# The keys' products of the mLSTM state placed directly behind the value products, in a two-layer hybrid encoder step

## The reference, cut to what matters

```
S   = einsum(q, k) * exp(D - m_t)
num = w_inter * einsum(C, q) + einsum(S, v)
den = w_inter * einsum(n, q) + sum(S)
h   = num / max(|den|, exp(-m_t))
w_s = exp(b_last - b + logi - m_new)
C_new = decay * C + einsum(w_s, v, k)
n_new = decay * n + einsum(w_s, k)
```

## Time and profile before

| what | value |
|---|---|
| median of 3 runs | 2419.7 us (2417.2 to 2423.41) |
| profiled execution, device time | 2419.36 us |
| its span, first to last instruction | 2417.6 us |
| granted TensorE clock, mean | 0.999 |
| PE busy | 2390.9 us (99%) |
| DVE, ACT, POOL busy | 1542.3 (64%), 1082.9 (45%), 524.5 us (22%) |
| mean DMA traffic | 111 GB/s |

### The profile page before, as it was taken

One profiled execution on the slowest core, in us unless ns is written; L12 is line 12 of the kernel. 1 busy time (PEld: TensorE's weight loads), 2 busy tenths in 40 slices (PEclk: granted clock), 3 DMA queues, 4 the chain that ended last, 5 costly groups with the idle time before them and its releaser, 6 DMA issues.

```text
span 2417.6 us, 42567 instructions
## 1 busy us (share of the span) xinstructions
PE 2390.9 (99%) x16827; PEld 2354.3 (97%) x16827; DVE 1542.3 (64%) x2733; ACT 1082.9 (45%) x2059; POOL 524.5 (22%) x578
## 2 busy tenths in 40 slices
PE   8999999999999999999999999999999999999998
PEld 8999988999999999999999999899999999999998
DVE  3115687888788877464611256878888887864464
ACT  6325666543333333343533356665433333333453
POOL 0001254422222220010110013443322222200110
PEclk9999999999999999999999999999999999999999
DMA  4442441212222223554624334312222222255564
GB/s 154 133 144 89 138 123 53 73 63 81 71 77 68 81 72 124 187 174 155 204 66 144 121 125 133 101 54 62 81 71 81 65 80 71 81 171 170 177 190 148
DMA packets 245177, 269.15 MB, mean 111 GB/s; under 512 B 16470, under 2 KB 215028, under 8 KB 242804
## 3 DMA queue, kind: packets, MB, share of 16 engines
q1 hardware_dynamic: 244980, 266.43, 35.0%
HBM read 216.27 MB, written 50.11 MB: 110 GB/s over the span
## 4 chain that ended last, share of the span: by engine, by line
PE 86%; DVE 6%; issue 3%; ACT 2%; POOL 1%; DVEq 0%; POOLq 0%; ACTq 0%
PE bank L327 27%; PE bank L329 27%; PE bank L328 27%; PE bank L1167 1%; PE bank L1177 1%; POOL wN L1946 1%; PE bank L1137 1%; PE bank L1092 0%; DVE mx L2179 0%; DVE hc L2258 0%; DVE xT L2102 0%; PE bank L1154 0%; DVE dec L2263 0%; DVE actL L444 0%; DVE wzL L2084 0%
## 5 line engine op out<-in xcount | busy, mean ns | idle before, releaser
L327 PE MATMUL bank<-actH,wb 128*128 128x384 f32 (+1 forms) x1712 | 560.1, 327 | 0.9 <-DVE actL L2333 0.6
L328 PE MATMUL bank<-actL,wb 128*128 128x384 f32 (+1 forms) x1712 | 554.9, 324 | 0.0
L329 PE MATMUL bank<-actH,wb 128*128 128x384 f32 (+1 forms) x1712 | 554.5, 324 | 0.0
L327 PE MATMUL bank<-wzH,actH 128*128 128x256 f32 (+3 forms) x1296 | 369.4, 285 | 3.6 <-DVE wzL L2059 1.9
L329 PE MATMUL bank<-wzH,actL 128*128 128x256 f32 (+3 forms) x1296 | 364.2, 281 | 0.0
L328 PE MATMUL bank<-wzL,actH 128*128 128x256 f32 (+3 forms) x1296 | 363.9, 281 | 0.0
L327 PEld LDWEIGHTS bank<-actH,wb 128*128 128x128 f32 x1712 | 322.4, 188 | 5.2 <-issue 2.8
L328 PEld LDWEIGHTS bank<-actL,wb 128*128 128x128 f32 x1712 | 323.1, 189 | 0.7
L329 PEld LDWEIGHTS bank<-actH,wb 128*128 128x128 f32 x1712 | 323.1, 189 | 0.0
L327 PEld LDWEIGHTS bank<-wzH,actH 128*128 128x128 f32 (+1 forms) x1296 | 236.3, 182 | 6.0 <-issue 2.4
L327 PE MATMUL bank<-tH,wb 128*128 128x384 f32 x704 | 237.7, 338 | 1.2 <-ACT vn L1860 1.2
(11 more groups left out here) (320 smaller groups left out, 5025.8 us busy)
## 6 DMA issues: line engine op xcount, KB each, us to landing
raw<-in_w_up SPq DMA_DIRECT2D x88, 512.0 KB, 4.6
raw<-in_w_down SPq DMA_DIRECT2D x88, 512.0 KB, 3.6
g_scratch<-cv SPq DMA_DIRECT2D x44, 545.0 KB, 3.2
rawz<-in_w_in SPq DMA_DIRECT2D x22, 1024.0 KB, 5.4
zb<-z_scratch SPq DMA_DIRECT2D x16, 1156.0 KB, 5.8
tHf<-g_scratch SPq DMA_DIRECT2D x88, 192.0 KB, 3.6
z_scratch<-zst SPq DMA_DIRECT2D x128, 128.0 KB, 1.8
raw<-in_w_out SPq DMA_DIRECT2D x128, 128.0 KB, 2.9
```

Of the source, the lines that this page charges most:

```text
L327: pe.matmul(out, aH, bH, start=first, stop=False)
L328: pe.matmul(out, aH, bL, start=False, stop=False)
L329: return pe.matmul(out, aL, bH, start=False, stop=last)
```

## The change

TensorE's stream in the seam is written in another order. The four keys' products (with their wait for `kw_r`) move from behind the turn of the gate row to directly behind the value products, ahead of `front_b` of the next block. The semaphore `kwmm_r`, which DVE and POOL wait for, is now set by the last product of line 1182 (`WTs` by `Vx`, line 1177 before), which ends later in the new order. `gate_rows` follows it, and then the filling. No instruction is added or removed, and no other engine's stream changes.

```diff
-                    if nx is not None:
-                        front_b(nx)
-
-                    pe.wait_ge(S["WTs_r"], b1)
+                    pe.wait_ge(S["kw_r"], b1)
                     pe.wait_ge(S["vx_r"], b1)
                     small(r)
                     for h in range(4):
-                        pe.matmul(bank[6][0:r, h * 65:h * 65 + 65], WTs[0:r, h, 0:r], Vx[0:r, h, :], start=True, stop=True)
+                        pe.matmul(bank[6][64 * (h % 2):64 * (h % 2) + 64, 260 + (h // 2) * 65:260 + (h // 2) * 65 + 65],
+                                  kw[0:r, h * 64:h * 64 + 64], Vx[0:r, h, :], start=True, stop=True)
+                    if nx is not None:
+                        front_b(nx)
+
+                    pe.wait_ge(S["WTs_r"], b1)
+                    small(r)
+                    for h in range(4):
+                        m = pe.matmul(bank[6][0:r, h * 65:h * 65 + 65], WTs[0:r, h, 0:r], Vx[0:r, h, :], start=True, stop=True)
+                    m.then_inc(S["kwmm_r"], 1)
                     if nx is not None:
                         gate_rows(nx)
 
-                    pe.wait_ge(S["kw_r"], b1)
-                    small(r)
-                    for h in range(4):
-                        m = pe.matmul(bank[6][64 * (h % 2):64 * (h % 2) + 64, 260 + (h // 2) * 65:260 + (h // 2) * 65 + 65],
-                                      kw[0:r, h * 64:h * 64 + 64], Vx[0:r, h, :], start=True, stop=True)
-                    m.then_inc(S["kwmm_r"], 1)
```

More of the change, by code:

```diff
@@ L1169, in back @@
                     m.then_inc(S["pv_r"], 1)
+                    pe.wait_ge(S["kw_r"], b1)
+                    pe.wait_ge(S["vx_r"], b1)
+                    small(r)
+                    for h in range(4):
+                        pe.matmul(bank[6][64 * (h % 2):64 * (h % 2) + 64, 260 + (h // 2) * 65:260 + (h // 2) * 65 + 65],
+                                  kw[0:r, h * 64:h * 64 + 64], Vx[0:r, h, :], start=True, stop=True)
                     if nx is not None:
@@ L1173, in back @@
                     pe.wait_ge(S["WTs_r"], b1)
-                    pe.wait_ge(S["vx_r"], b1)
                     small(r)
                     for h in range(4):
-                        pe.matmul(bank[6][0:r, h * 65:h * 65 + 65], WTs[0:r, h, 0:r], Vx[0:r, h, :], start=True, stop=True)
+                        m = pe.matmul(bank[6][0:r, h * 65:h * 65 + 65], WTs[0:r, h, 0:r], Vx[0:r, h, :], start=True, stop=True)
+                    m.then_inc(S["kwmm_r"], 1)
                     if nx is not None:
                         gate_rows(nx)
-                    pe.wait_ge(S["kw_r"], b1)
-                    small(r)
-                    for h in range(4):
-                        m = pe.matmul(bank[6][64 * (h % 2):64 * (h % 2) + 64, 260 + (h // 2) * 65:260 + (h // 2) * 65 + 65],
-                                      kw[0:r, h * 64:h * 64 + 64], Vx[0:r, h, :], start=True, stop=True)
-                    m.then_inc(S["kwmm_r"], 1)
                     dense(i, 6)
```

## The result

The changed kernel has a median of 2422.56 us in 22 runs (2419.96 to 2429.14), the kernel before beside it 2419.84 us in 22 runs (2415.8 to 2423.41). The ratio is 1.0014, 95% interval 1.0009 to 1.0020: 3.4 us more (the two medians themselves lie 2.7 us apart), slower by less than the 0.3% named ahead. The forecast was 2423.6 us.

What follows compares the result with a forecast made beforehand. TensorE, busy 99% of the span, was taken as the bound, DVE in middle seams. Per layer 2 x (-0.33) + 0 - 0.13 + 3 x 0.25 + 2.0 = +1.96 us, two layers +3.9; median 2423.6 us, range 2418.5 to 2429 us.

Steps and rivals of the forecast that it cites:

- The seams of blocks 0 and 1: Behind `aaw` 0.58 us removed, behind the value products 0.25 us added: -0.33 us a seam on TensorE.
- Block 2: Its seam: inserted 0.25 us hide behind a wait, TensorE's saving is not got back; 0, bounds -0.58 and +0.25 us.
- Block 3: Its seam: scores follow, so one change of array use stays; 0.38 us removed, 0.25 added, net -0.13 us.
- Blocks 4 to 6: Three seams bound by DVE's chain, +0.25 us each, +0.75 us a layer, bounds -0.4 and +2.6 us.
- So the chain that bounds these seams grows by the inserted 0.25 us: Blocks 4 to 6: DVE's `run` to `CN` comes 0.25 us later; TensorE's saving becomes a longer wait before 1073.
- a sign of being wrong: Prediction wrong if DVE's instructions between `nd` and `CN` take another total than 5.9 us in block 4.
- The worked-out reading of the skill's rule: Blocks 4 to 7: by exclusive SBUF ports, 2254 meets POOL's first addition and the chain lengthens by a whole one; 2429.6 us.
- DVE falls behind POOL: Rival, blocks 4 to 7: one more DVE instruction held, 0.75 us more a seam, 2429.6 us; chance 0.10.
- Block 7, the wait: TensorE waits for POOL's late `kw`: 1044 comes 2.27 us later, +2.0 us a layer passes through, bounds 1.5 and 2.5.
- I give back 0.25 us: Block 7: `rv` is no longer late for `vn`, so 0.25 us comes off; `run`, `nd`, `CN` 2.0 us later.
- The row speaks against it: Rival, block 7: clock falls to 1.2 GHz after the stall, 8 us more, 2431 us; dismissed by one row; chance 0.04.
- The rest of the kernel as it was: Outside the mixing stages, which were to lengthen by about 2 us each, the changed profile would show no difference.

Runs made afterwards that it cites:

- only7: Kernel before with the keys' products moved early in block 7 alone; 2428.16 us, ratio 1.0035 to the kernel before.
- keep7: Kernel before with the keys' products moved early in all blocks but block 7; 2417.14 us, ratio 0.9979 to the kernel before.
- kwfirst: Changed kernel with POOL's `kw` of block 7 written ahead of its two splits of w_out; 2416.35 us, ratio 0.9979 to the kernel before.
- again: The changed kernel once more, no edit, with a second profile; 2423.05 us, ratio 1.0007 to the kernel before.
- only4to6: Kernel before with the keys' products moved early in blocks 4, 5 and 6 alone; 2418.06 us, ratio 0.9994 to the kernel before.
- kwfirst2: Repeat of kwfirst (changed kernel, POOL's `kw` of block 7 ahead of its two splits); 2415.03 us, ratio 0.9981 to the kernel before.
- kwfirst_before: Kernel before, keys in the old place, with POOL's `kw` of block 7 ahead of its two splits; 2419.52 us, ratio 0.9999 to the kernel before.
- fill7_4: Changed kernel with four turns of the identity ahead of the wait for `kw` in block 7; 2421.4 us, ratio 1.0012 to the kernel before.

## Why the prediction was right, and where it was not

The total was right: 2423.6 us forecast, 2422.56 measured, +3.9 and +3.4 us. The mechanism named for it, the late `kw` of block 7, is what makes the kernel slower (`only7`, `keep7`, `kwfirst`). But that the number is so close is luck, since the total came out of errors that cancel: blocks 0 to 6 were put at -0.1 us in two layers and gained 3.8 in the profile, and the falls of the clock, worth about as much, were not in the sum.

*The seams of blocks 0 and 1: right.* -0.33 forecast, -0.32 to -0.41 measured; 0.58 removed and 0.25 added were 0.57 and 0.23.

*Block 2: taken at 0, it gained 0.24 and 0.46 us* (-0.01 and 0.24 in `again`; 0.25 in layer 1 of `only4to6`, where this block wasn't moved, so part of it is scatter). The step that failed is "what TensorE saves is not got back". The bound of -0.58 held it.

*Block 3: right in layer 0* (-0.13 forecast; -0.11 to -0.13 in seven of the nine profiles with the keys early there, but -1.20 in `kwfirst` and -0.69 in `kwfirst2`). Layer 1's -0.21 shows nothing, since this seam strays there by up to 1 us (+0.40 in `again`).

*Blocks 4 to 6: the wrong sign.* +0.25 a seam forecast, -0.09 to -0.49 measured but for one of +0.18. The step that failed is "So the chain that bounds these seams grows by the inserted 0.25 us". `run` comes later behind the value products, as forecast (0.23 us by the block mixer's start), but the chain behind it has no fixed length: it depends on which of DVE's instructions meet POOL's. From `nd` to `CN` it is 0.46 us shorter by the timelines in blocks 4 and 5 and 0.29 in block 6, in all ten profiles. In block 4 DVE's instructions from `nd` to the end of `CN` take 5.4 us where the text had 5.9, which it had named as a sign of being wrong. And block 6 isn't bound by this chain at all, but by TensorE, which the forecast had only as a bound. The text itself had warned of this in the rival (a shift may free one as well as hold one), and then let the chain stand at its old length. The worked-out reading of the skill's rule, that 2254 would meet the first addition, came true (0.86 us); that the chain would grow by a whole addition did not. In blocks 4 and 5 2255 went free in exchange, and `hc` was held for less. In block 6 2254 and 2255 were both held (0.86 and 0.65 us), and the two copies to `dec` (2263) took 0.87 us instead of 1.40, so the chain was shorter even so. The rival "DVE falls behind POOL" is thereby refuted for these blocks.

*Block 7, the wait: right in its size, wrong in its price.* The start of 1044 came 2.26 us later (2.27 forecast), though TensorE's idle time ahead of it was 1.82 us and not 2.0 to 2.1; 1.67 and 1.76 us at the end where 2.0 stood, inside the bounds of 1.5 to 2.5. "I give back 0.25 us" was too little, since 0.5 came back before the turn of `run`.

*Block 7, the clock: the step that failed is "The row speaks against it".* One row with one gap in which the clock stayed up was taken as a rule for all gaps and all executions; the rival got a chance of 0.04. The clock does fall behind this wait, to the 1.2 GHz level for 6.8 us, in about every second place where it could, by the estimate and by the profiles. One fall costs 3.0 us (4 us were worked out for the rival). The profiled execution of the changed kernel has none: who reads it alone finds -0.35 us in the mixing stages and never sees the clock.

*"The rest of the kernel as it was": wrong by 1.4 us a layer in the profiled execution.* POOL's sum and DVE's product in the feed-forward part exchanged places, by 0.46 us in layer 0 and by 0.14 in layer 1.

Put together for the median: block 7's wait +3.4 us in two layers; about 1.1 falls of the clock +3.4; blocks 0 to 6 -3.8. That makes +3.0, against +3.4 measured; with the -2.9 that blocks 0 to 6 have in `again` it would be +3.9, so the sum is good to about 1 us. The feed-forward step is left out of it, since the execution decides it too: the profile of `again` lacks it, though that is the changed kernel, and the profile of `kwfirst_before` has it, though TensorE's order there is that of before. Whether the change makes it more frequent is open: the profiles with early keys and without the added wait have it in 13 of 18 layers, those with the order of before in 2 of 6. How often it comes in the timed runs can't be seen.

Still open: what decides in which execution the clock falls after the same wait. The profiles show it falling after waits of 1.82 us, and not falling after others of 1.82 us. Open too is what puts POOL's sum ahead of DVE's product in some executions. The transfer of w_up isn't enough for it: in layer 0 the sum waited for its transfer in before and not in the changed kernel, but in layer 1 it waited for it in the changed kernel and not in before.

## What to carry to other kernels

- Before a wait is moved ahead of other work, look on the producing engine for the block in which its result comes last; one block in nine decided the sign here. Moving the producer (`kw` ahead of the splits) is then part of the same change: the early keys and the early `kw` were worth -0.21% together, +0.14% and 0.00% alone.
- A new wait of TensorE can cost more than its length, by a clock that falls behind it, and not in every execution: read the granted clock of all timed runs, not only that of the profile. If the wait can't be removed, idle matmuls in it can keep the clock up, as sixteen turns did here.
- Where VectorE and GpSimd both read SBUF, a shift of half a microsecond changes which instruction is held. A chain's length from the trace of before isn't then a constant; give such a term both signs.

## What the runs showed of the hardware that was not expected

- After a wait of TensorE of 1.8 us, the granted clock was at the 1.2 GHz level for 6.83 us in some executions (`again` in layer 0, `only7` in both layers) and at the full level in others (the changed kernel in both, `again` in layer 1). After four turns and a wait of 1.23 us it fell for as long (`fill7_4` in layer 1), and after 1.24 us it didn't (layer 0). A gap of 1.62 us ahead of block 4 never showed it. The engine ahead of the fall had 1.18 us of work in 3.00 (`again`, 392 to 395 us), or 1.77 (`fill7_4`, 1583 to 1586).
- Sixteen turns of the identity in the gap kept the mean granted clock at 0.9986 in 11 runs. The Trainium skill, TensorE: Matmul & The Clock Gate, "Part 4: PE-mode transpose", says that transposes don't count as busy for the clock in the same way. The trace lists these turns as MATMULs of 128x128, one for each turn where a product has two, and whether the page means this form no run here shows. Here they kept the clock up, and the measurement decides.
- Two instructions of POOL and DVE that start 0.02 us apart in one order, and 0.44 us apart in the other, take 1.29 and 2.42 us, or 2.02 and 1.29. The order decides: in all 15 places of the profiles without the added wait where POOL started 0.02 to 0.15 us ahead, DVE's took 2.29 us or more, and in all 9 where POOL started 0.01 to 0.44 us behind, DVE's took 1.29 or 1.30. That cost TensorE 1.4 us a layer, and one semaphore wait on POOL took it away.
